# First stage of a two-block transformer kernel rebuilt: constants and transposed input laid out ahead, the query latent kept feature-major, rotations out of PSUM by token halves, head scores summed on TensorE

## The reference

```
h = x @ w_in;  c_q, k, v, k_idx, w_idx = split(h, [256, 128, 128, 128, 8])
c_q = rms_norm(c_q, g_cq)
q = c_q @ w_uq (16 heads of 64);  q_idx = c_q @ w_iq (8 heads of 128)
k_idx = layer_norm(k_idx);  rope on q, k (16 of 64), q_idx, k_idx (32 of 128)
rel = relu(q_idx . k_idx) per index head;  score = sum over heads of w_idx * rel
score = -inf above the diagonal;  sel = top 64 keys of each query
attention of q over the selected k, v (2 key heads);  out @ w_o
```

## Time and profile before

| | us |
|---|---|
| three runs | 1234.02, 1237.85 (median), 1239.47 |
| the profiled execution, its own time | 1234.36 |
| its span, first to last instruction | 1232.2 |
| PE busy | 1112.5 (90%) |
| POOL busy | 829.6 (67%) |
| ACT busy | 551.1 (45%) |
| DVE busy | 471.4 (38%) |

### The profile page before, as it was taken

The page is one execution under the profiler, slowest core; times in us unless marked ns, Lnnn a source line. Parts: engine busy times, 40 slices in busy tenths (PEclk is TensorE's granted clock), DMA queues, the critical chain, the costliest instruction groups (busy, mean ns, idle before and its releaser), DMA issues.

```text
span 1232.2 us, 15620 instructions
## 1 busy us (share of the span) xinstructions
PE 1112.5 (90%) x6548; PEld 961.9 (78%) x6548; DVE 471.4 (38%) x854; ACT 551.1 (45%) x742; POOL 829.6 (67%) x299
## 2 busy tenths in 40 slices
PE   4675999999999966599999998999988898999997
PEld 4564787888889964477888888999988797788886
DVE  7559531114450779952111023260127525111102
ACT  3354544444335455444443425455563533543430
POOL 5243249978849757546987956978486274798880
PEclk9876999999999986699999999999998999999999
DMA  7210165555446530046555544554434143655540
GB/s 260 104 57 1 38 255 189 199 174 182 160 164 234 184 104 1 2 158 230 176 191 185 176 170 155 183 178 165 144 130 171 46 161 137 222 188 187 176 166 35
DMA packets 27952, 185.88 MB, mean 151 GB/s; under 512 B 3630, under 2 KB 4060, under 8 KB 6380
## 3 DMA queue, kind: packets, MB, share of 16 engines
q1 hardware_dynamic: 26156, 178.60, 41.2%
q10 hardware_dynamic: 1728, 6.29, 1.5%
HBM read 183.83 MB, written 1.05 MB: 150 GB/s over the span
## 4 chain that ended last, share of the span: by engine, by line
PE 78%; DVE 14%; ACT 3%; POOL 2%; issue 1%; DMA 1%; DVEq 0%
PE ps L350 24%; PE ps L352 24%; PE ps L351 24%; POOL wl L334 2%; DVE arena L1448 2%; DVE arena L468 1%; DVE arena L1449 1%; ACT wh L330 1%; PE ps L1114 1%; PE ps L1841 1%; DVE arena L1463 1%; PE ps L979 1%; DMA stage<-in_tiles 1%; DVE arena L783 1%; DVE arena L924 1%
## 5 line engine op out<-in xcount | busy, mean ns | idle before, releaser
L334 POOL TENSOR_TENSOR wl<-stage,wh 128x2048 fp32r<-128x2048 f32 x168 | 773.9, 4636 | 306.9 <-ACT wh L330 306.8
L330 ACT ACTIVATE wh<-stage 128x2048 fp32r<-128x2048 f32 x168 | 319.1, 1911 | 95.3 <-DMA stage<-in_tiles 94.3
L350 PE MATMUL ps<-wh,xh 128*128 128x512 f32 (+1 forms) x808 | 306.9, 380 | 18.2 <-POOL wl L334 5.9
L352 PE MATMUL ps<-wh,xl 128*128 128x512 f32 (+1 forms) x808 | 301.2, 373 | 0.0
L351 PE MATMUL ps<-wl,xh 128*128 128x512 f32 (+1 forms) x808 | 301.0, 372 | 0.0
L350 PEld LDWEIGHTS ps<-wh,xh 128*128 128x128 f32 x808 | 155.3, 192 | 48.4 <-issue 5.7
L350 PE MATMUL ps<-xh,wh 128*128 128x256 f32 x628 | 180.0, 287 | 8.6 <-DVE xl L1911 4.1
L351 PE MATMUL ps<-xl,wh 128*128 128x256 f32 x628 | 178.8, 285 | 0.0
L352 PE MATMUL ps<-xh,wl 128*128 128x256 f32 x628 | 178.7, 285 | 0.0
L352 PEld LDWEIGHTS ps<-wh,xl 128*128 128x128 f32 x808 | 155.2, 192 | 26.1
L351 PEld LDWEIGHTS ps<-wl,xh 128*128 128x128 f32 x808 | 155.6, 193 | 24.7 <-issue 0.5
(11 more groups left out here) (338 smaller groups left out, 1136.9 us busy)
## 6 DMA issues: line engine op xcount, KB each, us to landing
stage<-in_tiles SPq DMA_DIRECT2D x168, 1024.0 KB, 4.9
arena<-in_ln_g ACTq DMA_DIRECT2D x4, 512.0 KB, 3.5
arena<-in_ln_b ACTq DMA_DIRECT2D x4, 512.0 KB, 4.7
x_res<-in_x SPq DMA_DIRECT2D x1, 1024.0 KB, 5.1
out<-x_res SPq DMA_DIRECT2D x4, 256.0 KB, 2.0
arena<-in_pre_mix_norm ACTq DMA_DIRECT2D x1, 512.0 KB, 7.9
...
```

The lines of the kernel that those rows point to most:

```text
L330: nc.scalar.activation(wh[:, ring(n), :], stage[:, ring(n), :], ACT.Copy).then_inc(hi_done, 1)
L334: nc.gpsimd.tensor_tensor(wl[:, ring(n), :], stage[:, ring(n), :], wh[:, ring(n), :].bitcast(F32), ALU.subtract).then_inc(lo_done, 1)
L350: mm(out_, lh, rh, start=start, stop=False, skip_group_check=skip)
L352: return mm(out_, ll, rh, start=False, stop=stop, skip_group_check=skip)
```

## The change

The whole first stage is written anew; the attention itself and all behind it keep their code but for the few lines named last.

- The host lays x out transposed as well (`x_t`), and all small constants as one array `cst` of 327 columns. ACT's queue loads positions, `cst`, positions_2 and `wa`; SP loads x_t and tile 0 in halves, then tiles 1 to 5, then x.
- Tile order: index key and head weights (0), c_q (1), w_iq (2), k and v (3), w_uq (4). DVE, no longer POOL, makes the low parts of tiles 0 and 1.
- c_q comes out feature-major (tile 1 is the stationary operand), so it needs no transposes. Its gain is applied at once (to `hh[20..21]` and `hl[0..1]`); its row scale, from squares that PE sums, is applied later as a scalar of each rotation or copy.
- Only the 48 angle columns by two are reduced first, with scratch in PSUM; the second table's moved to `setup_dve2`, its sine to the start of `hgrn_act`, and so did the exponent of the HGRN bounds' inputs.
- Rotations of k, the index key, q_idx and the second half of q read PSUM (`rope_ps`) and put half of the products there; PE computes q_idx and q by token halves. POOL rotates only q's first half.
- The sum over heads is 16 matmuls by diagonal matrices `dw` of the head weights. q is computed and turned behind the scores; its second half is rotated after the sixth of eight top-k rounds. The mask passes through PSUM bank 7, once the turned q has been copied.
- ACT rounds tiles 9 and 10 ahead of the attention.

```diff
     w_att = A["att_w_in"][0]
-    for a in (0, 256, 648 - 256):
-        columns(w_att, a, 256)
+    columns(w_att, 648 - 256, 256)
+    columns(w_att, 0, 256)
     tiles.append(rows(A["att_w_iq"][0], 0, 2))
+    columns(w_att, 256, 256)
     tiles.append(rows(A["att_w_uq"][0], 0, 2))
...
+            if n == 0:
+                sp.dma_start(stage[:, 0, TW // 2:], A["tiles"][0, :, TW // 2:]).then_inc(stage_in[0], 16)
+                return
...
+        def low_ready(pe, n):
+
+            if n < 2:
+                pe.wait_ge(first_lo.sem, n + 2)
+            else:
+                pe.wait_ge(lo_done, n - 1)
...
+        def setup_loads(act):
+            nc.scalar.dma_start(pos_i, A["positions"], allow_slow_non_contiguous=True).then_inc(pos_in, 16)
+            nc.scalar.dma_start(cst[:], A["consts"]).then_inc(c_in, 16)
+            nc.scalar.dma_start(pos_t, A["positions_2"][0, :].partition_broadcast(P)).then_inc(late_in, 16)
+            nc.scalar.dma_start(wa[:], A["w_a2_2"][0]).then_inc(late_in, 16)
...
+        def reduce_angles(dve, x, n, width, between=None):
+
+            for c in range(2):
+                cols = slice(c * width, (c + 1) * width)
+                last = V.tensor_scalar(n[:, cols], x[:, cols], 1 / (2 * math.pi), 0.0 if c else 0.25, ALU.mult, ALU.add)
+            step(dve, last)
+            step(dve, V.tensor_scalar(n, n, MAGIC, MAGIC, ALU.add, ALU.subtract))
+            if between:
+                between()
+            for part in TURN:
+                step(dve, V.scalar_tensor_tensor(out=x, in0=n, scalar=-part, in1=x, op0=ALU.mult, op1=ALU.add))
+            step(dve, V.tensor_scalar(x[:, 0:width], x[:, 0:width], math.pi / 2, None, ALU.add))
+            return V.tensor_scalar(x, x, 3.1415925, -3.1415925, ALU.min, ALU.max)
+        def first_low(dve, part, signal, value):
+            dve.wait_ge(signal, value)
+            n = 1 if part == 2 else 0
+            c = slice(0, TW) if part == 2 else slice(part * (TW // 2), (part + 1) * (TW // 2))
+            V.tensor_tensor(wl[:, n, c], stage[:, n, c], wh[:, n, c].bitcast(F32), ALU.subtract
+            ).then_inc(first_lo.sem, first_lo.up())
...
         def setup_dve(dve):
-            dve.wait_ge(pos_in, 16 * 4)
+            for c in range(4):
+                x_lo(dve, c, x_raw)
+                if c == 1:
+                    first_low(dve, 0, first_hi.sem, 1)
+            first_low(dve, 1, hi_done, 1)
...
+            reduce_angles(dve, ang24.rearrange("p c f -> p (c f)"), ps[:, 2, 0:96], 48,
+                          lambda: first_low(dve, 2, hi_done, 2)).then_inc(reduced.sem, reduced.up())
+        def setup_dve2(dve):
             l0, l1, top = gt[:, 16:24], gt[:, 24:32], lb_x[:, 16:24]
-            V.tensor_tensor(top, l0, l1, ALU.max).then_inc(dve_step.sem, dve_step.up())
-            dve.wait_ge(dve_step.sem, dve_step.now())
-            V.tensor_tensor(lb_x[:, 0:8], l0, top, ALU.subtract).then_inc(dve_step.sem, dve_step.up())
+            step(dve, V.tensor_tensor(top, l0, l1, ALU.max))
+            V.tensor_tensor(lb_x[:, 0:8], l0, top, ALU.subtract)
             V.tensor_tensor(lb_x[:, 8:16], l1, top, ALU.subtract).then_inc(lb_in.sem, lb_in.up())
-
-
+            dve.wait_ge(late_in, 32)
+            step(dve, V.tensor_copy(trig_t[:, 1, :], pos_t))
+            step(dve, V.tensor_scalar(trig_t[:, 0, :], trig_t[:, 1, :], inv_t, None, ALU.mult))
+            step(dve, V.tensor_copy(trig_t[:, 1, :], trig_t[:, 0, :]))
+            reduce_angles(dve, trig_t[:, :, :].rearrange("p c t -> p (c t)"), ps[:, 6, :], T
+            ).then_inc(reduced_t.sem, reduced_t.up())
...
+        def rope_ps(dve, done, x, cos, sin, half, to, m_ps, m_sb, scale=None):
+
+            lo_, up = x[..., 0:half], x[..., half:2 * half]
+
+            def times(out_, y, c):
+                if scale is None:
+                    return V.tensor_tensor(out_, y, c, ALU.mult)
+                return V.scalar_tensor_tensor(out=out_, in0=y, scalar=scale, in1=c, op0=ALU.mult, op1=ALU.mult)
+
+            times(m_ps[0], lo_, cos)
+            times(m_sb[0], up, sin)
+            times(m_ps[1], up, cos)
+            step(dve, times(m_sb[1], lo_, sin))
+            V.tensor_tensor(to[..., 0:half], m_ps[0], m_sb[0], ALU.subtract)
+            V.tensor_tensor(to[..., half:2 * half], m_ps[1], m_sb[1], ALU.add).then_inc(done.sem, done.up())
...
+            pe.wait_ge(cq_ready.sem, cq_ready.due(pe))
+            query(2, 0, (4, 5)).then_inc(iq_ps.sem, iq_ps.up())
...
+            query(2, 1, (6, 7)).then_inc(used, 1)
+            index_turn(0)
...
+            tile_b(pe, 3, [(0, 0, ps[:, 2, 0:T])], done=False)
+            index_turn(1)
+            tile_b(pe, 3, [(1, 0, ps[:, 2, T:2 * T])])
...
+            pe.wait_ge(kr_done.sem, kr_done.due(pe))
+            for t, (bank, width) in enumerate(((2, P), (4, T))):
+                for h in range(IH):
+                    if h % (2 if t else 4) == 0:
+                        pe.wait_ge(relu_done.sem, relu_done.due(pe))
+                    last = mm(ps[:, bank, 0:width], dw[:, t * IH + h, :], relus[t][:, h, :], start=h == 0, stop=h == IH - 1)
+                last.then_inc(score_ps.sem, score_ps.up())
+                if t == 0:
+                    pe.wait_ge(kd_ready.sem, kd_ready.due(pe))
+                    for gr in range(KVH):
+                        for u in range(2):
+                            last = nc.tensor.transpose(ps[:, 0, gr * T + u * P:gr * T + (u + 1) * P],
+                                                       kd[:, u, gr, :, :].rearrange("p a b -> p (a b)"), ident[:])
+                    last.then_inc(kd_ps.sem, kd_ps.up())
+            query(4, 0, (1, 3)).then_inc(q_ps.sem, q_ps.up())
+            query(4, 1, (6, 7)).then_inc(used, 1)
+            pe.wait_ge(q_rot.sem, q_rot.due(pe))
+            pe.wait_ge(q1_done.sem, q1_done.due(pe))
+            pe.wait_ge(taken.sem, 2)
...
+            hi_until(act, 3)
...
+            index_plain(0)
+            index_plain(1)
+            index_turned(0)
             hi_until(act, 5)
-            act.wait_ge(lb_in.sem, lb_in.due(act))
-            nc.scalar.activation(lb_x[:, 0:16], lb_x[:, 0:16], ACT.Exp).then_inc(lb_exp.sem, lb_exp.up())
-            for c in range(4):
-                act.wait_ge(iqt_ps.sem, iqt_ps.due(act))
-                nc.scalar.activation(two(iqt, c), bank2(c), ACT.Copy).then_inc(iqt_done.sem, iqt_done.up())
+            index_turned(1)
+            hi_until(act, 6)
+            for b in range(2):
+                act.wait_ge(ix_ps.sem, ix_ps.due(act))
+                nc.scalar.activation(relus[0][:, 4 * b:4 * b + 4, :], bank4(4 + b), ACT.Relu
+                ).then_inc(relu_done.sem, relu_done.up())
+            for c, b in enumerate((1, 3, 6, 7)):
+                act.wait_ge(ix_ps.sem, ix_ps.due(act))
+                nc.scalar.activation(two(relus[1], c), bank2(b), ACT.Relu).then_inc(relu_done.sem, relu_done.up())
             hi_until(act, 8)
...
+            act.wait_ge(q_ps.sem, q_ps.due(act))
+            for c in range(2):
+                last = nc.scalar.activation(q[:, 0, c * 512:(c + 1) * 512], ps[:, 1 + 2 * c, :], ACT.Copy,
+                                            scale=small[:, 4:5])
+            last.then_inc(q_copied.sem, q_copied.up())
+            act.wait_ge(q1_rot.sem, q1_rot.due(act))
+            nc.scalar.activation(q[:, 1, :].rearrange("p (h f) -> p h f", h=HEADS)[:, :, 2 * ROT:],
+                                 heads_of(6, HD)[:, :, 2 * ROT:], ACT.Copy, scale=small[:, 5:6]
+            ).then_inc(q1_done.sem, q1_done.up())
+            hi_until(act, 10)
...
+                for h in range(IH):
+                    last = V.tensor_scalar(dw[:, t * IH + h, :], ident[:], wi[:, t, h:h + 1], None, ALU.mult)
...
+                if i == 5:
+                    dve.wait_ge(used, 5)
+                    c_, s_ = (x.unsqueeze(1).to_broadcast([P, HEADS, ROT]) for x in cs_q(1))
+                    m0 = [ps[:, 2, P * j:P * (j + 1)].rearrange("p (h f) -> p h f", h=HEADS) for j in range(2)]
+                    m1 = [tmp[:, j, 0:P].rearrange("p (h f) -> p h f", h=HEADS) for j in range(2)]
+                    rope_ps(dve, q1_rot, heads_of(6, HD), c_, s_, ROT,
+                            q[:, 1, :].rearrange("p (h f) -> p h f", h=HEADS), m0, m1, small[:, 5:6])
...
+            dve.wait_ge(qt_done.sem, 4)
+            mask = ps[:, 7, 0:3 * P]
+            step(dve, V.tensor_scalar(mask, score, TAKEN, -BIG, ALU.not_equal, ALU.mult))
+            V.tensor_copy(sbias[:, P:2 * P], mask[:, P:2 * P])
+            V.tensor_tensor(sbias[:].rearrange("p (c t) -> p c t", c=3)[:, 0:3:2, :],
+                            mask.rearrange("p (c t) -> p c t", c=3)[:, 0:3:2, :],
+                            causal.unsqueeze(1).to_broadcast([P, 2, P]), ALU.min).then_inc(sel_done.sem, sel_done.up())
...
         def hgrn_act(act):
+            act.wait_ge(reduced_t.sem, reduced_t.due(act))
```

(8 more changed lines are left out.)

453 lines of the change are left out of this document (199 added, 254 removed).

## The result

The changed kernel took 1203.22 us (median of four runs, 1199.56 to 1206.35), the kernel before 1235.97 on the same chip (1234.02 to 1239.47): a ratio of 0.9731, 95% interval 0.9687 to 0.9774, faster. Forecast were 1207 and a range of 1198 to 1222. The profiled execution took 1206.35 (span 1204.4) against 1234.36: 28.0 less, where the sum said 30.8.

The account below looks back on a forecast made before the run. PE was taken to bound the kernel (78% of the chain, DVE 14%). Top-k 36.6 us earlier less 7.0 given back is 29.6; with 1.2 more, 30.8 off the 1237.85 median gives 1207, range 1198 to 1222.

Parts of the forecast that it names:

- the sum: Whole kernel: top-k 36.6 us earlier, less 7.0 given back, plus 1.2 at 186, making 30.8 us less.
- Start: Kernel's start: first low half ready at 9, PE starting there instead of 19.92; tile 0 ends 17.5, tile 1 23.5.
- Angle: Ahead of the scores: four 96-column steps end at 17.0, two tensor_scalars beside POOL at 21.3, low latent at 27.8.
- Queries, keys, dw, kd: Latent to top-k: dw takes 3.5 to 4 us, done by 41.5; kd ends at 51.3; top-k starts at 58.6.
- Rival A: Before top-k: SBUF steps mostly collide with POOL, dw losing 9 to 14 us; about 1219; chance 0.17.
- D: Change does not reach top-k: PE's head sums cost 5.3 to 10.5; start, angle and 1.2 remain; 1223.5; chance 0.10.
- Rival B: Early gain hidden anyway: weight stream sets the end, earlier attention only waits for tiles; 1232 to 1238; chance 0.04.
- Given back 7.0: Behind top-k: first masked logits come 17.4 us after top-k starts instead of 10.4, returning 7.0 us.
- +1.2 at 186: At 186 us: tiles 9 and 10 converted ahead remove PE's 1.16 us wait on POOL, 1.2 us won.
- Moved block at nothing: Wide angle and exp, moved behind the feed-forward, cost nothing: 13.5 us added, 2.3 short of the cover.
- My sign for "wrong": At the HGRN boundary: the forecast is wrong if the first VectorE instruction has no wait on PE ahead.
- Rival C: Moved block runs over: 8 added steps wait for POOL, 45.6 and 4.3 us against 15.8 cover; 1241; chance 0.04.

Follow-up runs that it names:

- e2_angle_psum: Changed kernel with the narrow angle's last scaled step writing PSUM and both tensor_scalars and the sine reading there; 1198.33 us, ratio 0.9711 to the kernel before.
- e4_scores_dve: Changed kernel with the sum over index heads back on VectorE in SBUF, without the dw tiles and 16 matmuls; 1218.22 us, ratio 0.9876 to the kernel before.
- b1_const: Kernel before with ten constant loads replaced by one host-laid array and PE's transposes of them removed; 1233.51 us, ratio 0.9998 to the kernel before.
- e1: Changed kernel with ACT's roundings of tiles 9 and 10 put behind its four copies of the turned q; 1208.42 us, ratio 0.9793 to the kernel before.
- e8: Changed kernel with e2_angle_psum's edit, no 2-column copy behind the latent attention's second rotated query, and q's second half rotated after top-k round five; 1195.56 us.
- e6: Changed kernel with 20 more 512-column PSUM copies at the end of setup_dve2; 1221.99 us, ratio 0.9905 to the kernel before.

## Why the prediction was right, step by step

- **Reading.** The prediction calls 10.0 and 6.7 PE's two longest waits in the first 105.6 us; the longest was the 12.4 on L761, 11.4 of it in this stretch. Nothing in the sum rests on it.
- **Start.** Right in place: first low half at 9.82 (forecast 9), PE from 9.92. The second half came at 13.27 instead of 11.5, and PE ran at the lower level (0.21 us apart) until 19, so it starts tile 1 at 20.30, 2.8 later than said; with 48 more at 0.12 that ends at 26, not 23.5.
- **Angle.** The four steps took 1.13; of the two tensor_scalars behind them the addition (L486) took one hold and the clamp 0.21, ending at 22.8 (forecast 21.3). The row agrees with the Trainium skill's exclusive lock ("SBUF — State Buffer", section "SBUF: two separate sides"), and e2_angle_psum shows its other half: with PSUM ends the same steps are not held. cq_ready at 29.4 (forecast 27.8).
- **Queries, keys, dw, kd.** dw unheld, 3.23 us from 39.44, while POOL stood (36.5 to 43.2); kd one hold, done at 52.7. PE's transposes of kd at 52.96 followed its own sums (51.18 and 1.95 us), so that hold cost nothing. Top-k starts at 57.46 (forecast 58.6 with 2 us for a low clock): the granted clock was 0.94 between 28.5 and 57.5, so the allowance went to the later latent instead.
- **Rival A and D** fall: no stretch of several holds before top-k. But e4_scores_dve shows how near A was: one row put back into SBUF beside a fed POOL cost 13.8.
- **Rival B** falls, but it holds for a part: b1_const shows the host-laid constants alone hidden entirely.
- **Given back 7.0.** First masked logits 17.4 after top-k's start, as forecast to the tenth, with the idle time 4.24 (forecast 4.5). From the rotation's end to the last copy it took 6.5 (forecast 6.9). The account was half right: the roundings stand there, but taking them away (e1) shows that PE's slow turnings would have held the copies nearly as long. The 6.9 was about right as a sum and wrong as a lever: what moved the mask was rotating q one round earlier (e8).
- **+1.2 at 186**: wrong. PE still waits for POOL once, 1.1 us, between 110 and 240. In total its waits for POOL's low parts are 7.0 in 7, before 5.9 in 6.
- **Moved block at nothing**: right in the result, wrong in the working. I let two clamps lose a subtraction each, 13.5 in all; the block grew 16.8, since all eight subtractions that POOL began beside it held some step, where before it was five. (The old block had 27 instructions, not 32.) The cover was the 15.8, and 2.6 more between the layer norm's output (344.82 before) and PE's turning of it (347.44); the block also began 1.4 late against its reader (lead 28.8 against 30.3). 18.4 less 16.8 less 1.4 is what is left, 0.25 by the rows. My sign for "wrong" (no wait on PE ahead of L1090) was thus a bad sign: the wait that counts is PE's at L1044. Rival C falls: 16.8 us were added, not 49.9. Its 46.6 was the cover plus the whole gain, so that the change would turn slower; that point was not reached even in e6, 11.6 us under the kernel before. The cover itself was about 17, and e6's 14.6 on top cost 17.1, so my estimate from these is that the change would turn slower at some 41 us added.
- **Attention and all behind as long as before**: not quite. The attention takes 2.0 longer, 1.0 of it L818 beside POOL's tile 10, and the latent attention decides in each execution over 5.0 of the 6.7 us between a lead of 34.5 and one of 27.8 at the end.
- **The profiled difference** 28.0 against 30.8: at the first masked logits 30.7 were there against 29.6 forecast, so the working up to there holds. That the end is near the sum is in part luck: behind the masked logits the lead lost 1.9 in the attention, grew by 3.1 up to 700, and lost and regained until 27.8 were left, the upper group's 5 us the largest of these; the sum has none of them but +1.2, which did not come where it was put. The execution of the lower group is 34.7 under the profiled one of before. Why the lead grows behind the attention (in that one from 31.0 to 34.1 between 380 and 915) no run here isolates.
